# A token's expert rows joined in the expert loop instead of in a final pass (hybrid decoder layer, one core)

## What is computed

```python
y = grouped_experts(xn, eid.reshape(-1), wt.reshape(-1), w_gate, w_up, w_down)
# per expert: hid = silu(x @ w_gate[e]) * (x @ w_up[e]);  hid @ w_down[e], times the token's weight, summed per token
return h + y.reshape(b, s, d)
```

## Time and profile before

| | us |
|---|---|
| median of 3 runs (lowest to highest) | 1867.29 (1859.88 to 1869.38) |
| profiled execution: time | 1868.03 |
| profiled execution: span, first to last instruction | 1866.2 |
| PE busy over the span | 1737.6 (93%) |
| DVE busy | 1004.7 (54%) |
| ACT busy | 774.4 (41%) |
| POOL busy | 314.6 (17%) |
| mean granted TensorE clock | 0.961 |

### The profile page before, as it was taken

One profiled execution on the slowest core, in us unless ns is written; L12 is line 12 of the kernel. 1 busy time (PEld: TensorE's weight loads), 2 busy tenths in 40 slices (PEclk: granted clock), 3 DMA queues, 4 the chain that ended last, 5 costly groups with the idle time before them and its releaser, 6 DMA issues.

```text
span 1866.2 us, 28130 instructions
## 1 busy us (share of the span) xinstructions
PE 1737.6 (93%) x11006; PEld 1560.5 (84%) x11014; DVE 1004.7 (54%) x1392; ACT 774.4 (41%) x1038; POOL 314.6 (17%) x344
## 2 busy tenths in 40 slices
PE   6999999999989999999999799649999999999980
PEld 5999988999979999888899788548888888888870
DVE  6104211277743233212365433359988989989874
ACT  5222211233332233222311222227888878878760
POOL 0001200000111113110101400012333333333310
PEclk9999999999989989999999999769999999999995
DMA  5322332222223223443654322339999999999957
GB/s 182 125 90 99 131 122 78 74 91 83 80 84 116 77 78 107 130 149 118 195 214 129 99 91 91 153 126 359 376 383 376 389 389 391 394 383 391 387 214 292
DMA packets 122881, 365.55 MB, mean 196 GB/s; under 512 B 19089, under 2 KB 79057, under 8 KB 96578
## 3 DMA queue, kind: packets, MB, share of 16 engines
q1 hardware_dynamic: 102210, 312.76, 46.1%
q0 software_dynamic: 19344, 46.99, 6.8%
q10 hardware_dynamic: 1232, 4.46, 0.6%
HBM read 330.41 MB, written 68.52 MB: 214 GB/s over the span
## 4 chain that ended last, share of the span: by engine, by line
PE 91%; DVE 3%; DMA 3%; ACT 1%; issue 1%; POOL 0%; SPq 0%; DVEq 0%; POOLq 0%; ACTq 0%
PE ps L789 15%; PE ps L790 15%; PE ps L791 15%; PE ps L1171 6%; PE ps L1173 6%; PE ps L1172 6%; PE ps L1194 3%; PE ps L1196 3%; PE ps L1195 3%; PE ps L1027 2%; PE ps L964 2%; PE ps L938 2%; PE ps L1160 2%; DMA out_y_prompt<-part 1%; PE ps L1029 1%; PE ps L948 1%
## 5 line engine op out<-in xcount | busy, mean ns | idle before, releaser
L789 PE MATMUL ps<-part,part 128*128 128x256 f32 (+3 forms) x1912 | 610.1, 319 | 11.8 <-DVE part L1781 7.4
L790 PE MATMUL ps<-part,part 128*128 128x256 f32 (+3 forms) x1912 | 595.9, 312 | 0.0
L791 PE MATMUL ps<-part,part 128*128 128x256 f32 (+3 forms) x1912 | 595.6, 312 | 0.0
L1897 DVE TENSOR_TENSOR part<-part,part 128x2048 fp32r<-128x2048 f32 x192 | 440.0, 2293 | 61.7 <-ACT part L1454 57.6
L1454 ACT ACTIVATE part<-part 128x2048 fp32r<-128x2048 f32 x192 | 368.2, 1919 | 116.4 <-PE ps L1173 82.5
L789 PEld LDWEIGHTS ps<-part,part 128*128 128x128 f32 x1912 | 368.7, 193 | 20.9 <-DVE part L1781 9.1
L790 PEld LDWEIGHTS ps<-part,part 128*128 128x128 f32 x1912 | 368.8, 193 | 4.8
L791 PEld LDWEIGHTS ps<-part,part 128*128 128x128 f32 x1912 | 367.9, 192 | 5.1
L1171 PE MATMUL ps<-part,part 128*128 128x512 f32 x512 | 203.6, 398 | 3.5 <-DVE part L1947 3.5
L1173 PE MATMUL ps<-part,part 128*128 128x512 f32 x512 | 200.5, 392 | 0.0
L1172 PE MATMUL ps<-part,part 128*128 128x512 f32 x512 | 200.2, 391 | 0.0
(11 more groups left out here) (229 smaller groups left out, 2018.0 us busy)
## 6 DMA issues: line engine op xcount, KB each, us to landing
part<-w_gate SPq DMA_DIRECT2D x64, 1024.0 KB, 8.0
part<-w_up SPq DMA_DIRECT2D x64, 1024.0 KB, 7.5
part<-w_down SPq DMA_DIRECT2D x64, 1024.0 KB, 7.3
part<-w_in SPq DMA_DIRECT2D x25, 1024.0 KB, 5.4
part<-x_prompt SPq DMA_DIRECT2D x16, 512.0 KB, 3.5
part<-expert_out_scratch SPq DMA_DIRECT2D x8, 1024.0 KB, 6.7
gate_scratch<-part POOLq DMA_DIRECT2D x32, 192.0 KB, 3.0
part<-gate_scratch SPq DMA_DIRECT2D x4, 1088.0 KB, 6.4
```

What stands on the lines that cost most here:

```text
L789: mm(out, lhs[0](k), rhs[0](k), start=(k == 0), stop=False)
L790: mm(out, lhs[0](k), rhs[1](k), start=False, stop=False)
L791: last = mm(out, lhs[1](k), rhs[0](k), start=False, stop=(k == n - 1))
L1897: tt(elo[:, off % NSPL, :], eraw[:, off % NRAW, :], ehi[:, off % NSPL, :].bitcast(F32), ALU.subtract)\
```

## The change

The final pass, y_d, ACT's y_evac and the output stores of ACT are gone. For each token the expert with the lower block number is its first, the other its second. Two DRAM scratches replace y_d: h_d holds h, and y1_d takes the first expert's rows (both are filled with h while h is made, 18 more stores of up to 512 KB on POOL). For each expert:

- POOL clears a buffer (memset 128x1024) and gathers into it h for the rows for which this expert is the second one (`residual`);
- DVE forms weight times PSUM output plus that buffer (`y_weigh`, scalar_tensor_tensor of 128x1024; one input in PSUM, one in SBUF), between its sixth c_lo and hid_lo;
- POOL scatters the first-expert rows to y1_d (`store_first`), gathers for the second-expert rows what their first expert left (`load_first`), adds it (`add`, a tensor_tensor of 128x1024 with both inputs in SBUF, one expert late), and scatters the sums to the prompt output and to the sample output (`store_rows`, two indirect DMAs).

The last expert's add is made by DVE. The index columns are used in place, without the small copies. The weights reach the row layout through a second table product (18 more small matmuls, float32) and DVE gets four small operations ahead of `onehot` and about ten behind `table_ready`. Raw slots: 10 instead of 6, of which the sixth to eighth wait for the stores of h and the last two for `table_ready` and the first gather. The loops of SP, ACT, DVE and POOL over the experts are written out; PE keeps its loop. In the diff, the overflow path and the renamed counters are left out.

```diff
-    y_d = dram("expert_out_scratch", [2 * T, D])
+    h_d = dram("h_scratch", [T, D])
+    y1_d = dram("first_expert_scratch", [T, D])
...
-    NRAW, NSPL = 6, 3
+    NRAW, NSPL, EARLY = 10, 3, 8
...
+    eraw += [Lay(AFTER_M + 2 * D + CW * i).take(CW) for i in range(EARLY - 5)]
+    eraw += [Lay(AFTER_W + CW * i).take(CW) for i in range(NRAW - EARLY)]
...
+                c = 6 * b + off
+                if c == 5:
+                    sp.wait_ge(s("h_st"), 32 * TILES)
+                if c == EARLY:
+                    sp.wait_ge(s("table_ready"), 2)
+                    sp.wait_ge(s("xg_in"), 16)
+                if c >= NRAW:
+                    sp.wait_ge(s("e_split"), c - NRAW + 1)
+                load_chunk(kind, j, expert, c % NRAW)
...
+        pe.wait_ge(s("onehot"), 2)
+        for i in range(2 * TILES):
+            last = mm(ps[:, 3, 2 * SLOTB:3 * SLOTB], in_row[:, i, :].bitcast(F32), w_col[:, i, :], start=(i == 0), stop=(i == 2 * TILES - 1))
         last.then_inc(s("tab_mm"), 1)
...
         x_tr(0)
+        pe.wait_ge(s("table_ready"), 2)
         gate_up(0, first_chunks(), 0)
...
-            y_evac(b - 1, b * 6 + 4, first=(bn == 1))
             hid_hi(b)
...
-        for t in range(TILES):
-            act.wait_ge(s("yo_ready"), t + 1)
-            if t == ST:
-                dst, src = o["y_sample"].rearrange("b s d -> (b s) d"), yo[t % 2][0:NSAMP, :]
-            else:
-                dst, src = o["y_prompt"][0, P * t:P * t + P, :], yo[t % 2]
-            act.dma_start(dst, src).then_inc(s(f"y_out{t % 2}"), 16)
...
+        step(tt(second[:, :, 0], R["blkf"][:, :, 0], R["blkf"][:, :, 1], ALU.is_gt))
+        step(tt(second[:, :, 1], R["blkf"][:, :, 1], R["blkf"][:, :, 0], ALU.is_gt))
+        step(tt(second, second, cst[:, CVALID:CVALID + TILES].unsqueeze(2).to_broadcast([P, TILES, 2]), ALU.mult))
+        ids = second.rearrange("p t j -> p (t j)")
+        step(tt(ids, ids, cst[:, CID:CID + 2 * TILES], ALU.add))
+        tt(num_col, in_col, ids.unsqueeze(2).to_broadcast([P, 2 * TILES, SLOTB]), ALU.mult)\
...
+        step(tt(wts_v, wts[:, :, :], cst[:, CVALID:CVALID + TILES].unsqueeze(2).to_broadcast([P, TILES, 2]), ALU.mult))
+        tt(w_col, in_col, wts_v.rearrange("p t j -> p (t j)").unsqueeze(2).to_broadcast([P, 2 * TILES, SLOTB]), ALU.mult)\
+            .then_inc(s("onehot"), 1)
...
+        dve.wait_ge(s("tab_mm"), 2)
+        cp(wtab[:, :], ps[:, 3, 2 * SLOTB:3 * SLOTB]).then_inc(s("table_ready"), 1)
...
+        def y_weigh(b, used):
+            dve.wait_ge(s("e_used"), used)
+            dve.wait_ge(s("h_in"), 16 * b + 16)
+            if b >= 2:
+                dve.wait_ge(s("low_st"), 16 * (b - 1))
+                dve.wait_ge(s("y_sum"), b - 1)
+            stt(yw[b % 2], flat(5)[:, 0:D], wtab[:, b:b + 1], hg[b % 2], ALU.mult, ALU.add).then_inc(s("y_read"), 1)
...
+            y_weigh(b - 1, b * 6 + 4)
             hid_lo(b)
...
+        y_weigh(NE - 1, 6 * NE)
+        dve.wait_ge(s("y_read"), NE)
+        dve.wait_ge(s("y1_in"), 16 * NE)
+        tt(y1[(NE - 1) % 2], y1[(NE - 1) % 2], yw[(NE - 1) % 2], ALU.add).then_inc(s("y_sum"), 1)
...
+            dma(h_d[col0(t):col0(t) + w, :], hbuf[0:w, t, :]).then_inc(s("h_st"), 16)
+            dma(y1_d[col0(t):col0(t) + w, :], hbuf[0:w, t, :]).then_inc(s("h_st"), 16)
...
+        def residual(i, idx, k):
+            nc.gpsimd.memset(hg[i], 0.0).then_inc(s("zeroed"), 1)
+            pool.wait_ge(s("zeroed"), 4 + k)
+            pool.indirect_dma_start(hg[i], None, h_d, at(idx), bounds_check=T - 1, oob_is_err=False).then_inc(s("h_in"), 16)
+
+        def store_first(i, idx):
+            pool.indirect_dma_start(y1_d, at(idx), yw[i], None, bounds_check=T - 1, oob_is_err=False).then_inc(s("low_st"), 16)
+
+        def load_first(i, idx):
+            pool.indirect_dma_start(y1[i], None, y1_d, at(idx), bounds_check=T - 1, oob_is_err=False).then_inc(s("y1_in"), 16)
+
+        def add(i):
+            nc.gpsimd.tensor_tensor(y1[i], y1[i], yw[i], ALU.add).then_inc(s("y_sum"), 1)
+
+        def store_rows(i, idx_p, idx_s):
+            pool.indirect_dma_start(y_p, at(idx_p), y1[i], None, bounds_check=NPROMPT - 1, oob_is_err=False).then_inc(s("y_st"), 16)
+            pool.indirect_dma_start(y_s, at(idx_s), y1[i], None, bounds_check=NSAMP - 1, oob_is_err=False).then_inc(s("y_st"), 16)
+
+        def load_first_of(b):
+            if b > 0:
+                pool.wait_ge(s("low_st"), 16 * b)
+            if b >= 2:
+                pool.wait_ge(s("y_st"), 32 * (b - 1))
+            load_first(b % 2, tabh[:, b:b + 1])
+
+        def finish_sum(b):
+            pool.wait_ge(s("y1_in"), 16 * (b + 1))
+            add(b % 2)
+            pool.wait_ge(s("y_sum"), b + 1)
+
+        gather(tabt[:, 0:1])
+        pool.wait_ge(s("xg_tr"), 1)
+        gather(tabt[:, 1:2])
+        pool.wait_ge(s("table_ready"), 2)
+        residual(0, tabh[:, 0:1], 1)
+        pool.wait_ge(s("xg_tr"), 2)
+        gather(tabt[:, 2:3])
+        pool.wait_ge(s("h_in"), 16)
+        residual(1, tabh[:, 1:2], 2)
+        for b in range(NE):
+            if b + 3 < NE:
+                pool.wait_ge(s("xg_tr"), b + 3)
+                gather(tabt[:, b + 3:b + 4])
+            if b == NE - 1:
+                finish_sum(b - 1)
+                load_first_of(b)
+                store_rows((b - 1) % 2, tabp[:, b - 1:b], tabh[:, b - 1:b])
             pool.wait_ge(s("y_read"), b + 1)
-            nc.gpsimd.tensor_copy(idxy[:, 0:1], tabs[:, bass.ds(b, 1)]).then_inc(s("idx_ready"), 1)
-            pool.wait_ge(s("idx_ready"), k + 1)
-            pool.sem_inc(s("index_used"), 1)
-            pool.indirect_dma_start(y_d, bass.IndirectOffsetOnAxis(ap=idxy[:, 0:1], axis=0), yb, None,
-                                    bounds_check=2 * T - 1, oob_is_err=False).then_inc(s("y_st"), 16)
-
-        gather(0, 0)
-        for b in range(1, 3):
-            pool.wait_ge(s("xg_tr"), b)
-            gather(b, b)
-        with pool.Fori(3, NE) as b:
-            pool.wait_ge(s("xg_tr"), b)
-            gather(b, b * 2 - 3)
-            store(b - 3, b * 2 - 2)
-        for i in range(3):
-            store(NE - 3 + i, 2 * NE - 3 + i)
+            if 0 < b < NE - 1:
+                pool.wait_ge(s("low_st"), 16 * b)
+            if b == NE - 1:
+                pool.wait_ge(s("y1_in"), 16 * NE)
+            store_first(b % 2, tabl[:, b:b + 1])
+            if b + 2 < NE:
+                pool.wait_ge(s("h_in"), 16 * (b + 2))
+                residual(b % 2, tabh[:, b + 2:b + 3], b + 3)
+            if b < NE - 1:
+                if b > 0:
+                    finish_sum(b - 1)
+                load_first_of(b)
+                if b > 0:
+                    store_rows((b - 1) % 2, tabp[:, b - 1:b], tabh[:, b - 1:b])
+        pool.wait_ge(s("y_sum"), NE)
+        store_rows((NE - 1) % 2, tabp[:, NE - 1:NE], tabh[:, NE - 1:NE])
```

More of the change, by code:

```diff
@@ L334, in _build @@
     num_col = lr.take(2 * TILES, SLOTB, dt=F32R)
+    wts_v = lr.take(TILES, 2)
+    second = lr.take(TILES, 2)
+    w_col = in_col
     assert lr.at <= AFTER_M
-    NRAW, NSPL = 6, 3
+    NRAW, NSPL, EARLY = 10, 3, 8
     CW = 2048
     le_ = Lay(0)
-    eraw = le_.take(NRAW, CW)
     ehi = le_.take(NSPL, CW, dt=F32R)
     elo = le_.take(NSPL, CW, dt=F32R)
+    eraw = [le_.take(CW) for _ in range(5)]
+    assert le_.at <= 2 * KT * T + WSLOT + 4 * D
     xg = le_.take(D)
@@ L1466, in hid_hi @@
             act_(hTh, ps[:, 4, :].rearrange("p (k n) -> p k n", n=P), ACT.Copy).then_inc(s("hid_hi"), 1)
-        def y_evac(b, used, first=False):
-            act.wait_ge(s("e_used"), used)
-            if not first:
-                act.wait_ge(s("y_st"), b * 16)
-            act_(yb, flat(5)[:, 0:D], ACT.Copy).then_inc(s("y_read"), 1)
         act.wait_ge(s("x2_st0"), 16 * 5)
@@ L1485, in _, with turn @@
         hid_hi(0)
-        def turn(b, bn, last=False):
+        def turn(b):
             for off in (1, 2, 3, 4):
@@ L1491, in turn @@
             silu(b, b * 6 + 2)
-            if not last:
+            if b + 1 < NE:
                 xg_hi(b + 1)
             c_hi(b, 5)
-            if not last:
+            if b + 1 < NE:
                 c_hi(b, 6)
-            y_evac(b - 1, b * 6 + 4, first=(bn == 1))
             hid_hi(b)
-        turn(1, 1)
-        with act.Fori(2, NE - 1) as b:
-            turn(b, None)
-        turn(NE - 1, None, last=True)
-        y_evac(NE - 1, 6 * NE)
+        for b in range(1, NE):
+            turn(b)
         act.wait_ge(s("table_ready"), 1)
@@ L1978, in turn @@
                 c_lo(b, 6)
+            y_weigh(b - 1, b * 6 + 4)
             hid_lo(b)
-        with dve.Fori(1, NE - 1) as b:
-            turn(b)
-        turn(NE - 1, last=True)
+        for b in range(1, NE):
+            turn(b, last=(b == NE - 1))
+        y_weigh(NE - 1, 6 * NE)
+        dve.wait_ge(s("y_read"), NE)
+        dve.wait_ge(s("y1_in"), 16 * NE)
+        tt(y1[(NE - 1) % 2], y1[(NE - 1) % 2], yw[(NE - 1) % 2], ALU.add).then_inc(s("y_sum"), 1)
```

(17 more changed lines are left out.)

124 lines of the change are left out of this document (75 added, 49 removed).

## The result

The changed kernel took 1936.7 us (median; 1931.3 to 1941.0) beside 1864.2 us of the kernel before on the same chip: 1.037 times as long [1.035, 1.040]. The prediction said 1886 us with a range up to 1922. The direction was right, the size was not.

The account below looks back on a forecast made before the run. PE bounds the expert stage at 17.75 us a turn, DVE just behind; a serial chain of 50.4 us ends it. Span 1866.2 + 46.5 (turns) - 29 (end) + 1.5 (start) = 1885.2, forecast 1886 us, range 1839 to 1922.

Parts of the forecast that it names:

- The bound of the kernel before: Expert stage: PE sets the turn at 17.75 us, DVE just behind with 16.1 us of work a turn.
- y_weigh: DVE in the turn: 1.23 us more, 16.7 us in all, which by itself fits into 17.75.
- The hold: DVE in the turn: POOL's add of about 2.6 us blocks a running c_lo for 2.5 us.
- DVE's turn of 19.2: Expert stage: DVE's 16.7 us of work plus 2.5 us blocked by POOL's add make 19.2 us.
- POOL's turn: Expert stage: 13.9 us of POOL operations plus 5.4 us of waits beside c_lo's, 19.3 us a turn (16 to 22).
- The step that failed: Expert stage: DVE's 19.2 and POOL's 19.3 taken as a turn of 19.3 us, 1.55 x 30 = +46.5 us.
- The third rival: Expert stage: late gathers stall x_tr and c_lo's shift into the add, 20.5 us a turn, 1922; 0.17 with the fourth.
- the fourth: End: POOL's queue replaces the long end, a backlog of 15 us, 1900 us; chance 0.17 together with the third.
- The first rival: Expert stage: the add falls where nobody minds, PE keeps 17.75 or 18.1 us, 1840 to 1850; chance 0.28.
- The second: Expert stage: DMA is the bound, 7.13 MB take 18.5 us a turn, 1862 us; 0.17 with what lies between.
- The end: After the last matmul: POOL's chain replaces the 50.4 us of scatter, reload, multiply and store, -29 us.
- The start: Before the first expert: second float32 table product and four small DVE operations, +1.5 us (-3 to +5).

Follow-up runs that it names:

- before_evac_dve: The kernel before with the evacuation of an expert's output (128x1024 from PSUM) on VectorE in place of ScalarE: 17.76 us a turn, ratio 1.003.
- before_with_add: The kernel before with one GpSimd add of 128x1024 a turn on buffers nobody else uses: 19.01 us a turn, 1904 us.
- gather_early: The changed kernel with the next expert's gather right behind GpSimd's add, ahead of the load of first rows and the output's stores: 19.79 us a turn, 1899.6 us.
- no_add: The changed kernel with GpSimd's add cut from 1024 columns to 8: 20.29 us a turn, 1916.6 us.
- interleaved: The changed kernel with experts in order 0, 8, 16, 24, 1, ..., first rows added in y_weigh, no GpSimd add or memset: 18.22 us a turn, 1844.9 us.
- gather_early_no_add: The changed kernel with the next gather right behind GpSimd's add and that add cut from 1024 columns to 8: 18.64 us a turn, 1868.8 us.
- both moved: The changed kernel with the add on VectorE, one expert late, and the next gather ahead of the output's stores: 18.94 us a turn.
- memset_for_add: The changed kernel with GpSimd's add replaced by an add of 8 columns and a memset of 2700 columns of an unread buffer: 21.97 us a turn.
- add_twice: The changed kernel with a second GpSimd add of 128x1024 each turn, into a buffer nobody reads: 23.22 us a turn.
- add_on_dve: The changed kernel with the add of 128x1024 moved from GpSimd to VectorE, one expert late: 19.37 us a turn, 1888 us.

## Why the prediction came out as it did

**The bound of the kernel before** and **y_weigh** were right: y_weigh took 1.27 us (1.23 taken), and is free by itself (before_evac_dve).

**The hold** was right in kind and nearly in size: 2.40 us for the add (2.6 estimated), a c_lo of 4.90 (up to 4.8 was said). Over the whole stage the mean c_lo was 2634 ns, 192 x 0.34 = 66 us in all, from 25 held ones (over 3.3 us) for 31 adds. The Trainium skill, "SBUF — State Buffer", section "SBUF: two separate sides", describes it, and before_with_add measures it: 2.7 us a turn. For the add itself the estimate from the Trainium skill, "GPSIMD Engine Reference", section 3.1 (2.3 us) was nearer than my proportion from short adds (2.6), whose fixed part I had scaled up with the rest. DVE's turn of 19.2 became 19.8, as its gaps don't vanish when it is full.

**POOL's turn** of 19.3 was right only by parts that cancel. Indirect DMAs follow one another with 0.30 us between them, not 0.6; the memset took 0.98 (1.0); but four of the six issues shown took 2.3 to 2.9 us beside a c_lo, and a mean of 0.8 for such waits was too little for them. From store to store it was 20.15 with POOL loaded, 1.07 of it a wait.

**The step that failed** is "DVE's 19.2 and POOL's 19.3 agree by chance. I take 19.3 a turn". It took the turn for the greatest of three engines' work, with no path across them. The runs showed two bounds in its place, both above 19.3. One is a latency: POOL's chain from store to gather, the landing, and PE and DVE up to the next y_weigh but one, 40.8 and 44.5 us for two turns in the rounds read (the mean turn of 20.87 asks for 41.7). The other is DVE's turn with the hold and its gaps, 19.8 once the ring is short (gather_early). With the hold gone and the ring left it is 20.29 (no_add), with both gone 18.64. In the changed kernel the two take turns, and the lower clock behind PE's waits adds up to 0.5 us. The ring's three lengths could have been had from the traces of before: about 17 us of POOL's 19.3 lie ahead of the gather, 10.0 of landing, and from x_tr, which began at 1500.20 in that turn, to POOL's release by y_evac at 1509.76 it is 9.6, some 12 with y_weigh's place behind a c_lo. That makes 39 for two turns, 19.5 each, with no wait of DVE or PE for anything else. The third rival named this ("Gathers land late because POOL waits for c_lo's, x_tr then stalls PE") and priced it at 20.5 us and 1922, but let it begin at a POOL turn of 19.5 us and gave it, together with the fourth, 0.17. It has no such threshold: it depends on where in POOL's chain the gather stands. gather_early showed that, with 1.1 us a turn for a move that saves no work. This term of the sum was +46.5 and measured +90.4.

**The first rival** fell by both bounds, each enough for it, and the fourth by the end, which did get shorter. **The second** was wrong here (340 GB/s, six slots the same) and fits interleaved and gather_early_no_add: whoever removes the other two seems to meet it at 18.2 to 18.6 us.

**The end** was -29 and measured -21. POOL took up store_first(30) at 1903.03, 30.8 us behind x_tr(31) (26 predicted). Its chain to the end of the last issue was shorter, 20.3 against 24.3 us, thanks to the 0.30 us. But from there to the end of the span it was 9.5 us, where I had 2.2:

```profile
1919.45 1.34 POOL L2152 DMA_INDIRECT first_expert_scratch<-part,part  x1 [1.31 <-DMA part<-first_expert_scratch,part]
1921.10 0.97 POOL L2161 DMA_INDIRECT out_y_prompt<-part,part  x1 [0.30 <-issue]
1922.38 0.98 POOL L2162 DMA_INDIRECT out_y_sample<-part,part  x1 [0.30 <-issue]
```

The landings of the two last stores' kinds take 2.6 and 3.4 us there, and the rest of the 9.5 has no record. Interleaved has 6.8 us between the end of its last issue and the end of its span. What fills this time isn't shown.

**The start** was +1.5 (-3 to +5) and measured -2.5. Over all kernels x_tr(2) starts between 1261.5 and 1271.1, so nothing is to be read in it.

## What to carry to other kernels

When work is added to an engine that also issues transfers for a later step, don't compare engine totals alone: follow the new instructions from what releases them to the last transfer issued behind them, add the landing and the way back to the releaser, and divide by the number of turns that the ring spans. An issue that others wait for goes ahead of the ones that nobody waits for; here that move alone gave back 37 of the 72 us. Two bounds of nearly the same size hide each other, and each experiment that removes one shows only the difference to the next: the ring some 20.9 us a turn, the hold 19.8, 18.9 with both moved (not settled), full DMA queues 18.2 to 18.6, TensorE 17.75.

## What the runs showed of the hardware

- Back-to-back indirect DMAs on GpSimd start 0.30 us after the one before ends; one behind a result of GpSimd itself 0.80 us, one behind a VectorE result 1.07 to 1.20.
- An indirect DMA's instruction takes 0.97 to 1.04 us, and up to 3.1 beside a c_lo (one of 192 in the changed kernel has 5.1). An add of only 8 columns took 1.70 us in the mean in memset_for_add and 0.82 in gather_early_no_add. A memset of 1024 columns took 0.98 us with or without a c_lo beside it, one of 2700 took 2.35, and neither lengthened a c_lo (2289 ns in the mean of no_add, 2.29 to 2.40 beside the long memset).
- With gaps in its work TensorE's granted clock fell in some windows: 0.98 in the changed kernel at 1500 to 1600 us, 0.93 in no_add, 0.88 in add_twice. In interleaved, 98.8% busy in that window, it was 1.00, but so it was in add_on_dve with 92.6%: there PE's longest wait in 1280 to 1780 us was 2.0 us, in the changed kernel 5.6. Once it fell, what it costs shows in the matmuls: 0.63 us each and 0.42 apart at 0.50, 0.39 and 0.23 at 1.00.
